# First gate pair of four modulated feed-forward blocks computed in two halves, one of them before the norm's scale is known

## What is computed

```python
mod = silu(c) @ ada_w[l] + ada_b[l]                  # nine vectors of 1024: shift, scale, gate, three times
h = rms_norm(x, norm_ffn1[l]) * (1 + sc1) + sh1
x = x + 0.5 * g1 * swiglu_2(h, ffn1_w_in[l], ffn1_w_out[l])
h = rms_norm(x, norm_mix[l]) * (1 + sc2) + sh2
x = x + g2 * token_mix(h, ...)
h = rms_norm(x, norm_ffn2[l]) * (1 + sc3) + sh3
x = x + 0.5 * g3 * swiglu_2(h, ffn2_w_in[l], ffn2_w_out[l])
```

## Time and profile before

| | |
|---|---|
| median of 3 runs | 3123.5 us (3122.21 to 3124.0) |
| the profiled execution | 3121.7 us, of which the span from first to last instruction is 3120.0 us |
| mean granted TensorE clock | 0.99 of full speed |
| busy: TensorE, VectorE, ScalarE | 98%, 56%, 38% of the span |

### The profile page before, as it was taken

How to read it: one execution, slowest core, us unless ns; L and a number is a source line. 1 busy time by engine, 2 the same in 40 slices (tenths; PEclk the granted TensorE clock), 3 DMA queues, 4 the chain that set the end, 5 groups by cost and what they waited for, 6 DMA issues and landing times.

```text
span 3120.0 us, 39735 instructions
## 1 busy us (share of the span) xinstructions
PE 3049.3 (98%) x14471; PEld 2518.8 (81%) x14471; DVE 1744.7 (56%) x2766; ACT 1189.8 (38%) x1706; POOL 125.7 (4%) x117
## 2 busy tenths in 40 slices
PE   8999999989999999999999999999999999999998
PEld 6788888877888888888877888888888888788887
DVE  6577524765776256642688666324333478743323
ACT  3433323465233234432345444324443244644422
POOL 0000000000000000000030000000000003000000
PEclk9999999999999999999999999999999999999999
DMA  3355333213554335633321365322333322122332
GB/s 126 123 189 188 108 100 91 88 41 109 180 179 148 99 101 184 199 98 95 93 82 55 116 199 184 98 94 88 96 99 94 102 79 82 41 88 94 98 104 74
DMA packets 262908, 351.35 MB, mean 113 GB/s; under 512 B 16664, under 2 KB 208536, under 8 KB 262808
## 3 DMA queue, kind: packets, MB, share of 16 engines
q1 hardware_dynamic: 240768, 270.57, 27.8%
q0 software_dynamic: 21360, 79.01, 7.8%
q10 hardware_dynamic: 680, 0.44, 0.0%
HBM read 348.76 MB, written 2.10 MB: 112 GB/s over the span
## 4 chain that ended last, share of the span: by engine, by line
PE 86%; DVE 9%; ACT 3%; issue 2%; DMA 0%; POOL 0%; DVEq 0%; SPq 0%; ACTq 0%
PE bank L1834 27%; PE bank L1836 26%; PE bank L1835 26%; DVE w_lo L1097 1%; ACT w_hi L650 1%; PE bank L1857 1%; DVE work L1148 1%; PE bank L1860 1%; PE bank L1858 1%; DVE a_score L1435 1%; DVE h_lo L1154 1%; DVE sumsq L1110 0%; PE bank L1912 0%; PE bank L1908 0%; ACT probs L967 0%
## 5 line engine op out<-in xcount | busy, mean ns | idle before, releaser
L1097 DVE TENSOR_TENSOR w_lo<-raw,w_hi 128x1024 fp32r<-128x1024 f32 x482 | 589.7, 1224 | 1166.6 <-ACT w_hi L650 1165.9
L650 ACT ACTIVATE w_hi<-raw 128x1024 fp32r<-128x1024 f32 x508 | 538.1, 1059 | 1364.4 <-PE bank L1836 1334.8
L1834 PE MATMUL bank<-h_hi,w_hi 128*128 128x512 f32 x2656 | 1043.2, 393 | 10.1 <-DVE w_lo L1097 6.8
L1836 PE MATMUL bank<-h_hi,w_lo 128*128 128x512 f32 x2656 | 1035.9, 390 | 0.0
L1835 PE MATMUL bank<-h_lo,w_hi 128*128 128x512 f32 x2656 | 1035.7, 390 | 0.0
L1834 PEld LDWEIGHTS bank<-h_hi,w_hi 128*128 128x128 f32 x2656 | 499.8, 188 | 119.3 <-DVE w_lo L1097 8.7
L1836 PEld LDWEIGHTS bank<-h_hi,w_lo 128*128 128x128 f32 x2656 | 499.7, 188 | 105.5
L1835 PEld LDWEIGHTS bank<-h_lo,w_hi 128*128 128x128 f32 x2656 | 500.0, 188 | 101.4
L1834 PE MATMUL bank<-act_hi,w_hi 128*128 (+1 forms) x1120 | 435.9, 389 | 1.0 <-DVE w_lo L1097 1.0
L1836 PE MATMUL bank<-act_hi,w_lo 128*128 (+1 forms) x1120 | 435.7, 389 | 0.0
L1835 PE MATMUL bank<-act_lo,w_hi 128*128 (+1 forms) x1120 | 435.7, 389 | 0.0
(11 more groups left out here) (315 smaller groups left out, 2647.1 us busy)
## 6 DMA issues: line engine op xcount, KB each, us to landing
raw<-in_ffn_w_in_dram SPq DMA_DIRECT2D x176, 512.0 KB, 3.5
ada_w<-in_ada_w_dram POOLq DMA_DIRECT2D x72, 1024.0 KB, 5.6
raw<-in_ffn_w_out_dram SPq DMA_DIRECT2D x88, 512.0 KB, 3.6
raw<-in_ffn_w_gate_dram SPq DMA_DIRECT2D x44, 512.0 KB, 3.9
raw<-in_ffn_w_up_dram SPq DMA_DIRECT2D x44, 512.0 KB, 3.9
raw<-in_ffn_w_down_dram SPq DMA_DIRECT2D x44, 512.0 KB, 3.7
raw<-in_mix_w_in_dram SPq DMA_DIRECT2D x44, 512.0 KB, 3.6
raw<-in_attn_w_qkv_dram SPq DMA_DIRECT2D x24, 512.0 KB, 3.6
```

The lines of the kernel that those rows point to most:

```text
L650: nc.scalar.activation(w_hi[:, nb % SPL, :], raw[:, nb % RAW, :], ACT.Copy).then_inc(s_hi, 1)
L1097: V.tensor_tensor(w_lo[:, nb % SPL, :], raw[:, nb % RAW, :], w_hi[:, nb % SPL, :].bitcast(F32), ALU.subtract).then_inc(s_lo, 1)
L1834: T.matmul(dst, wh, mh, start=first, stop=False)
L1836: return T.matmul(dst, wl, mh, start=False, stop=last)
```

## The change

It concerns the four norms q = 5, 7, 8, 10 and the first iteration of the four blocks behind them.

- As the residual chunks 0 to 3 are finished, ScalarE and VectorE also make the hi and lo parts of x * gain of these chunks, without rstd and shift (`early_hi`, `early_lo`). In a feed-forward block this is in steps 12 to 15 of the down product, in an output phase beside chunks 0 to 4.
- In the hole TensorE runs the first gate slab on them: eight units of three matmuls into banks 4 and 5 (`early_units`), five ahead of the sums, one behind them, two at the end. The fillers go. Between the spreading and the last two units come 16 fp32 matmuls with one moving column (`shift_products`): the same slab times the shift, since the shift isn't scaled by rstd.
- `norm_tail` goes through chunks 4 to 7 first, then 0 to 3. After the first four VectorE copies the shift's products out of bank 2, ScalarE and VectorE split slab 2, and ScalarE copies banks 4 and 5 into `sq`.
- TensorE runs the second gate slab on chunks 4 to 7 into banks 0 and 1 (`later_half`), then the up pair in order of chunks.
- VectorE puts the halves together (`two_halves`): early half times rstd, plus the shift's products, plus the later half, four instructions of 512 columns. ScalarE's silu reads the result. On VectorE this stands behind the split of slab 3 and ahead of `ada_half` 0.
- The first iteration is written out ahead of the loops on ScalarE and VectorE.

```diff
+            def early_hi(q, k):
+                _, l, n, _, _ = EARLY[q]
+                nc.scalar.activation(h_hi[:, k, :], xT[:, k, :], ACT.Identity, scale=coefs[:, l, n, k:k + 1]).then_inc(s_hhi, 1)
...
+                turn = 4 if q in EARLY else 0
+                for p in range(KC + 1):
...
+                    if q in EARLY and p == 3:
+                        dve.wait_ge(s_shiftmm, EARLY[q][4] - 1)
+                        V.tensor_copy(shifted[:], bank[2][:, 0:2]).then_inc(s_shift, 1)
+                    if q in EARLY and p == 4:
+                        split_lo(N0[f"ffn{EARLY[q][4]}"] + 2)
...
+            def two_halves(f):
+                nb, rstd = N0[f"ffn{f}"], bank[6]
+                dve.wait_ge(s_used, nb + 2)
+                for c in range(2):
+                    dve.wait_ge(s_early, 2 * (f - 2) + c + 1)
+                    link(V.tensor_tensor(work[:, c, :], sq[:, c, :], rstd[:], ALU.mult))
+                    dve.wait_ge(s_shift, f - 1)
+                    V.scalar_tensor_tensor(out=work[:, c, :], in0=work[:, c, :], scalar=shifted[:, c:c + 1], in1=bank[c][:],
+                                           op0=ALU.add, op1=ALU.add).then_inc(s_gate, 1)
...
                 def body(i, ada, first=False):
-                    split_lo(nb + 2, i)
+                    if f < 2 or not first:
+                        split_lo(nb + 2, i)
+                    if f >= 2 and first:
+                        split_lo(nb + 3, i)
+                        two_halves(f)
                     if ada:
                         ada_half(i, 0)
-                    split_lo(nb + 3, i)
+                    if f < 2 or not first:
+                        split_lo(nb + 3, i)
...
+            def shift_products(q):
+                _, l, _, shift, f = EARLY[q]
+                wh, wl = slab(N0[f"ffn{f}"], 256)
+                pe.wait_ge(s_mod, 18 * (l + 1))
+                for c in range(2):
+                    at = slice(c * P, (c + 1) * P)
+                    for k in range(4):
+                        col = mod[:, shift + k:shift + k + 1]
+                        T.matmul(bank[2][:, c:c + 1], wh[:, k, at].bitcast(F32), col, start=c == 0 and k == 0, stop=False)
+                        ins = T.matmul(bank[2][:, c:c + 1], wl[:, k, at].bitcast(F32), col, start=False, stop=c == 1 and k == 3)
+                ins.then_inc(s_shiftmm, 1)
...
             def mean(q):
 
                 pe.wait_ge(s_x, 8 * (4 if q == 5 else q) + 4)
+                if q in EARLY:
+                    early_units(q, 0, 5)
+                    square_sums(4 if q == 5 else q)
+                    early_units(q, 5, 6)
+                    spread(q)
+                    shift_products(q)
+                    early_units(q, 6, 8).then_inc(s_used, 1)
+                    return
                 keep_warm(9)
```

More of the change, by code:

```diff
@@ L168, in program @@
         scratch1 = place("scratch1", [P, 1])
+        shifted = place("shifted", [P, 2])
         ada_cols = place("ada_cols", [P, S // 32])
@@ L713, in residual_squares @@
                         gained_hi(q, k)
+                    if q in EARLY_AT and k < 4:
+                        early_hi(EARLY_AT[q], k)
             def ffn(f, q_next):
@@ L1143, in norm_tail @@
                 base, ht = H0[hname], HT0[hname]
[L1144 to L1148, removed]
-                                               in1=rstd[:], op0=ALU.mult, op1=ALU.mult).then_inc(s_htmp, 1)
-                    if k:
-                        c = k - 1
-                        dve.wait_ge(s_hhi, base + c + 1)
-                        sh = 0.0 if shift is None else mod[:, shift + c:shift + c + 1]
-                        V.scalar_tensor_tensor(out=h_lo[:, c, :], in0=work[:, c % 4, :], scalar=sh,
+                turn = 4 if q in EARLY else 0
@@ new lines, in norm_tail @@
+                for p in range(KC + 1):
+                    if p < KC:
+                        k = (p + turn) % KC
+                        if p >= 4:
+                            dve.wait_ge(s_hlo, base + p - 3)
+                        V.scalar_tensor_tensor(out=work[:, p % 4, :], in0=xT[:, k, :], scalar=gains[:, k:k + 1],
+                                               in1=rstd[:], op0=ALU.mult, op1=ALU.mult).then_inc(s_htmp, 1)
+                    if p:
+                        c = (p - 1 + turn) % KC
+                        dve.wait_ge(s_hhi, base + p)
+                        V.scalar_tensor_tensor(out=h_lo[:, c, :], in0=work[:, (p - 1) % 4, :], scalar=mod[:, shift + c:shift + c + 1],
@@ L1180, in body @@
                 def body(i, ada, first=False):
-                    split_lo(nb + 2, i)
+                    if f < 2 or not first:
[3 more added lines that the diff above has]
+                        two_halves(f)
                     if ada:
                         ada_half(i, 0)
-                    split_lo(nb + 3, i)
-                    if first:
+                    if f < 2 or not first:
+                        split_lo(nb + 3, i)
+                    if first and f < 2:
                         rstd_columns(2 * f + 1)
@@ L1236, in ffn @@
                 else:
-                    with dve.Fori(0, NF // 2) as i:
+                    with dve.Fori(1, NF // 2) as i:
                         body(i, False)
@@ L1945, in body @@
                         pe.wait_ge(s_x, 8 * q + 6)
-                    if first:
+                    if first and f >= 2:
+                        later_half(f, hname)
+                    elif first:
                         first_pair(nb, (0, 1), h_hi, h_lo, H0[hname], H0[hname])
@@ L1951, in body @@
                         pe.wait_ge(s_dveT, dt + 2 * i)
-                    if first and f < 2:
+                    if first and f >= 2:
+                        pe.wait_ge(s_shift, f - 1)
+                        half_pair(nb + 2, 0, (2, 3), h_hi, h_lo, (s_hlo, H0[hname] + 4))
+                        half_pair(nb + 2, 1, (2, 3), h_hi, h_lo)
+                    elif first and f < 2:
                         square_sums(q)
```

84 lines of the change are left out of this document (63 added, 21 removed).

## The result

| | before | after |
|---|---|---|
| median of 15 runs (range), us | 3122.95 (3121.26 to 3125.74) | 3128.93 (3128.06 to 3132.93) |
| ratio, 95% interval | | 1.0021 (1.0014 to 1.0028) |
| profiled execution, us | 3121.7 | 3128.36 |
| its span, us; mean granted clock | 3120.0; 0.99 | 3126.7; 0.988 |

The kernel became slower by 6.0 us, 0.2%. The forecast was 3133.6 in a range of 3121 to 3140.

A forecast was written before the change was run, and what follows sets the result against it. The prediction took TensorE, busy 98% of the span, as the bound, with gains only in its holes. Path -14.1, VectorE stalls +8.3 and clock +17.7 on 3121.7 gave 3133.6 us, range 3121 to 3140.

The forecast's parts named there:

- TensorE's own path at full clock: From the first early unit to the first up product in the four holes: 14.1 us gained in all.
- The bound for the shift's calls: The 16 single-column shift products in each hole: 0.227 us a call, 3.63 us, taken from the sums' records.
- Hole 1's 19.8: Path at full clock to the first up product at q = 5: 19.8 us against 26.2, 6.4 gained.
- The clock: In all four holes it falls 6 to 8 us after the hole's start; 17.7 us lost, bounds 0 and 23.
- my two bounds: Length of a hole's stretch at clock 0.50: about 7.8 us, between 6.6 and 10.2.
- Rival 1: The clock holds in all four holes: 3115.9 us, faster; with brief falls 3122.6, no change. Chance 0.20.
- VectorE's queue: End of first iteration, f = 2 and 3: slab 4 late, TensorE stalls 4.3 and 4.0 us, 8.3 lost.
- Rival 2: VectorE isn't late: the 8.3 us stall is absent or hidden in the clock's stretches, 3125.3 us, no change. Chance 0.12.
- The sum: Whole kernel, from the profiled execution: 3121.7 - 14.1 + 8.3 + 17.7 = 3133.6 us.
- my clock terms: The holes' clock losses, 3 x 3.9 + 6.0 us, taken as means over chances, so nothing was added to the total.
- Rival 3: Early parts slow the output phases of q = 7 and 10 by 1.5 us each, low stretches longest: 3141.9. Chance 0.08.

The follow-up runs named there:

- experiment 2: Changed kernel with the shift's single-column calls mixed among the early units, sums and spreading instead of one block, same instructions in the holes: 3123.81 us, ratio 0.9999 to before.
- experiment 1: Changed kernel with 14 of the 16 shift calls of each hole left out: 3117.94 us, ratio 0.9986 to the kernel before.
- 1b: The changed kernel without 14 of the 16 shift calls of each hole, unchanged repeat of experiment 1, one profile: 3121.06 us.
- 2b: The changed kernel with the mixed order of units and shift calls, unchanged repeat of experiment 2, one profile: 3122.62 us.
- experiment 4: Changed kernel with the shift split once into rounded parts, each call having both as two moving columns, VectorE adding the results: 3123.78 us, ratio 1.0005 to before.
- experiment 6: Changed kernel with the nine modulation steps of f = 2 and 3 in iterations 1 to 9 instead of 0 to 8: 3116.16 us, ratio 0.9979 to before.
- experiment 5: Changed kernel with `ada_half` 0 of the first iteration of f = 2 and 3 moved ahead of the norm's tail: 3123.11 us, ratio 0.9999 to before.
- 7: The kernel of experiment 6 with the mixed order of units and shift calls in holes 2 to 4 alone: 3110.52 us, ratio 0.9960 to before.

## Why the prediction held, point by point

**TensorE's own path at full clock: held in holes 2 to 4.** 17.1, 16.8 and 17.1 us were worked out for holes 2 to 4; experiment 2, with the same instructions and the clock at 1.00, has U at 17.22, 16.82 and 17.22. The bound for the shift's calls, taken from the sums' records, was 0.227 a call, measured 0.223. The sums in holes 2 and 4 start 3.53 us after T0, 0.13 behind the five units and not 0.3. Hole 1's 19.8 has no test of its own, since no run of that order kept the clock there.

**The clock: right in kind; right in sum by two errors that cancel.** U less the path worked out is 2.6, 4.7, 4.8 and 4.7 us, in sum 16.8 where 17.7 stood. In holes 2 to 4 the low stretch began 7.2 to 7.5 us after T0 and lasted 10.2, the upper of my two bounds, where I took 7.8 (3.9 lost each). I let the clock come back 2 to 3 us after the last two units begin; it took 4.8 to 5.3 (hole 3: 2140.85 to 2146.2). That is 2.5 us more lost in three holes than I had. In hole 1 I had 6.0 and it was 2.6: I let the sums lie in the low stretch, but it began behind them, and the clock came back for most of the shift's calls. That is 3.4 us less. So the sum is near by luck. Experiments 1 and 1b take the calls away, and with them every fall ahead of U in holes 2 to 4 (hole 1 keeps one of 3.4 us, right behind its sums); experiments 2 and 2b keep them and are at 0.50 for 0 or 3.4 us there. Rival 1, the clock that holds, is ruled out for this kernel by two profiles. The Trainium skill (TensorE: Matmul & The Clock Gate, Part 1) has the clock follow how busy the engine has been. Read by busy time, the runs don't agree: 10.10 of 10.10 us busy at 0.50 in the changed kernel, with 7.20 of 7.20 busy from T0 to the fall, and 13.95 of 15.40 at 1.00 in experiment 1. The rows that the prediction used for this were weaker: ahead of the low stretch of hole 1 before, TensorE had been idle for 1.57 us.

**VectorE's queue: right, a little too high.** Stalls of 4.3 and 4.0 us were expected, 4.1 and 3.1 came, and none in f = 4 and 5. By V the working can be tested: 17.1 + 14.9 = 32.0 for hole 2 against 31.93 in experiments 1 and 4, where the clock held, and 19.8 + 15.2 = 35.0 for hole 1 against 35.33, with one low stretch of 3.4 us. (The 2.4 us by which the tail was to end behind U is more than the prediction's own 19.0 less 16.8 or 17.1.)

That the stalls add to the clock's loss, as the sum has it, is not shown there and needed a reason. With V of hole 2 set by VectorE at 32 us, a TensorE that is 4.7 us late would first have used up the stall. It didn't, since VectorE waited for the slowed TensorE too. VectorE of the changed kernel in hole 2:

```profile
1766.05 0.16 DVE L1180 COPY shifted<-bank 128x2 f32<-128x2 f32 x1 [1.05 <-PE bank L2005]
1769.99 1.23 DVE L1117 TENSOR_TENSOR w_lo<-raw,w_hi 128x1024 fp32r<-128x1024 f32 x1 [2.46 <-ACT w_hi L658]
```

The copy waits for the last shift call, and the split of slab 2 for ScalarE's rounding, which needs the first slab used up by units 6 and 7. These 3.5 us are absent in experiments 1, 2 and 4, and they are most of the 3.8 by which V of hole 2 lies behind 31.93. What I missed beside it is what follows a gap: the clock falls in dense products behind it, 1.7 us lost in f = 2. Rival 2, a VectorE that isn't late, is out; its share of 57% says nothing of one stretch with a fixed order. Experiment 6 prices the whole: the two stalls, the low stretch behind one of them, and shorter low stretches in holes 2 to 4, together 12.8 us of median.

**The sum.** Against the profiled execution before, in us: the path -14.1 as predicted; the clock +16.8 for 17.7; the stalls +7.2 for 8.3; and -0.9 that I left out, since before the change the 48 up products took 11.0 to 11.2 and not 10.88. Together +9.0 for +11.9. Outside the terms lie +1.7 behind the gap, -3.3 in the two untouched holes and -0.7 of rest. That gives 3128.4 where 3133.6 was forecast. The median, 3128.93, is clear of the kernel before, but it lies under the 3129.7 from which the prediction spoke of slower by over 0.2%. The largest part of the miss, the -3.3, is in no step of the prediction: I had said that my clock terms were means over chances, but had given the holes of q = 6 and 9 none. It came in both profiles of the changed kernel, but there is one profile of the kernel before, and one and the same kernel can differ there: V of q = 6 was 31.06 in experiment 2 and 32.67 in 2b. So how much of the -3.3 is the change's isn't known, nor why these two holes keep their clock in some profiles and not in others (V at 32.65 and about 31.04 in experiments 1 and 1b).

**Rival 3,** the output phases slowed by 1.5 us, didn't come: the sums' input was there 3.5 us after T0 in hole 2, before the 3.7 expected. The whole output phase ahead of it, from V of q = 6 to T0 of hole 2, took 214.1 us (214.0 before), and the stretch with the down products, from V of hole 2 to T0 of hole 3, 339.65 in both: the early parts are free.

**What stays open.** How long the clock stays low once it falls: the same block of calls in hole 3 gave 10.2 us in the changed kernel and 3.4 in experiment 6, with the same instructions on TensorE from T0 to U. The traces show a part of it: the clock came back 2.8 to 5.3 us after units 6 and 7 began, in holes 2 to 4 of the changed kernel (both profiles) and of experiments 5 and 6, so the later it fell, the shorter it was low. A fall 6.2 us after T0 gave 13.7 us, falls at 6.8 to 7.5 gave 10.2, at 8.7 and 9.3 gave 6.8, at 9.7 and 9.8 gave 3.4. What sets the time of the fall is open. Also not tried: the early halves in some of the holes only, and experiment 6's shift of the modulation on the kernel before. The latter has no stall in its first iteration, so I'd expect little of it, but that is argued and not shown.

## What to carry to other kernels

Filling a hole of the bottleneck engine pays in full only if what fills it keeps the clock. In these runs single-column matmuls between wide ones kept it more often than in one block, so look at the granted clock and not at the busy share. Work that moves out of the hole onto a second engine joins that engine's fixed order, so add up its queue from the end of the norm to the next thing that the first engine needs, and move out of it whatever isn't due (here one modulation step in each of two blocks, which ended stalls of 4.1 and 3.1 us; the rest of its 12.8 us came with shorter low stretches). With all of this and cheaper calls, a change that had lost 6 us gained 22.

## What the hardware did that I had not expected

- An idle gap brings the clock down for what comes after it. Behind 3.9 us without work in experiments 1 and 4, and behind 2.8 in the changed kernel's f = 2, dense 512-column products ran at 0.50; behind the 1.8 of its f = 3 they didn't. But no length of gap can be read off as a limit: experiment 2's f = 2 has the same two waits as that f = 3, 1.80 and 0.74 us, and its next product is at 0.50:

```profile
1172.59 0.80 PE L1886 MATMUL bank<-h_hi,w_hi 128*128 128x512 f32 x1 [0.74 <-DVE w_lo L1117]
```

A longer gap, TensorE of experiment 4 at the end of the first iteration of f = 3:

```profile
1783.51 0.39 PE L1901 MATMUL bank<-h_hi,w_lo 128*128 128x512 f32 x1
1787.82 0.61 PE L2082 MATMUL bank<-ada_cols,squares 128*128 128x16 f32 x2 [3.93 <-DVE ada_cols L1262]
1788.96 0.80 PE L1899 MATMUL bank<-h_hi,w_hi 128*128 128x512 f32 x1 [0.52 <-DVE w_lo L1124]
1789.55 0.63 PE L1900 MATMUL bank<-h_lo,w_hi 128*128 128x512 f32 x1
```

- The falls of some kernels repeat: to 0.1 us in holes 2 to 4 of the changed kernel and in all holes of experiment 1. Those of the mixed order don't (hole 1 was at 0.50 for 17.1 us in experiment 2 and for 3.4 in 2b). With the fp32 calls in one block the clock was low in 12 of 12 of holes 2 to 4 (the changed kernel twice, experiments 5 and 6), for 3.4 to 13.7 us. In 11 of them it fell in the block or right at its end; in hole 2 of experiment 5 it fell before the block began. Mixed, it held in 6 of 9 (experiments 2, 2b and 7) and fell for 3.4 us in the other three.
- An fp32 matmul with one moving column is two records and 0.22 us. With rounded operands and two columns, so twice the data, it is one record and 0.11 us.
